# A weighted sum over a large table: two half rows per load instead of one

## Chip, cores and metric

The kernel runs on one core of a Trainium2 chip. The metric is the device time of one execution in microseconds (us). Three timed executions of the kernel before gave a median of 1765.91 us (1764.79 to 1768.8). A separate execution was profiled; its own time stands in the table further down.

## What is computed

One transformer-like block works on 512 tokens of width 1024. Its second half, where the change lies, is a retrieval over 16384 "experts": a row of table `u_tab` and a row of table `v_tab` each, 1024 numbers wide, 64 MB a table. Cut from the reference:

```python
e_idx = ...            # 8 heads x 16 chosen experts per token
gates = jax.nn.softmax(cv, axis=-1)
def one_block(args):
    xi, ei, gi = args
    ue = jnp.take(u_tab, ei, axis=0)
    a = jnp.einsum('thkd,td->thk', ue, xi)
    wgt = (jax.nn.gelu(a.astype(jnp.float32)) * gi).astype(xi.dtype)
    ve = jnp.take(v_tab, ei, axis=0)
    return jnp.einsum('thk,thkd->td', wgt, ve)
```

## The kernel before, in words

For 384 of the 512 tokens the kernel does the retrieval densely. The 128 other tokens get their rows by indirect loads. A table has 128 **chunks** of 128 experts. The *first product* multiplies a chunk of `u_t` with all tokens (PE, TensorE) and gives gelu(u x) in `gelz`. The gates, scattered earlier into a DRAM array `gates_by_key`, come back by loads into `gring` (four chunks a load, 768 KB, line 499). `weigh` (DVE, line 1449) multiplies the two into `wf`. The *second product* multiplies `wf` with the chunk of `v_tab` and adds up in PSUM.

The matmuls work on 32-bit numbers split into a high and a low part. A raw tile is copied to its high part on ACT (`part_v`, line 890, `vhi`; `part_w`, line 882, `eh`), and DVE takes the difference (`low_v`, line 1461, `vlo`; `low_w`, line 1455, `el`). PE then multiplies high by high, low by high and high by low (lines 1629 to 1631).

The second product runs in 16 **groups** g of 8 chunks. PSUM holds only half of the 1024 output columns at a time, so a group does its 8 chunks for the left half of the columns, and then again for the right half. This gives 16 **pieces** n = 0..15 in a group: n = 8 * half + k. A piece needs a tile of 128 experts by 512 columns of `v_tab` (256 KB) and is 9 matmuls on PE. The raw tiles lie in `vraw`, a ring of VR = 4 buffers; `vhi` and `vlo` are rings of 4 too. In groups 0 to 4 PE also does a first product ahead of each of the pieces 0 to 7 (`PRE`, first_product in `group`). From group 5 (`V_GROUP`) on it does sums of indirectly loaded rows instead (`quad`, line 1908, tile `ring`): three of them a group, and four a group in groups 5 and 6. These rows are loaded by POOL (line 654), four loads of 512 KB each time that a quad has freed the buffers.

Each engine takes its own list of instructions in order, and semaphores join them. SP issues nearly all loads; the list is:

- `first_half(g)`: for k = 0..7 the load of piece k; behind the loads of even k a load of `gback` (384 KB, line 507, gelu values that were written out earlier; from group 6 on); behind those of k = 0 and 4 a load of `gring`.
- `second_half(g)`: the loads of pieces 8..15, with the loads of `u_t` for the next group between them as long as there are chunks left.

The `gring` load behind piece 0 of group g, called the **seam load** here, brings the gates of the group's chunks 4 to 7. DVE needs it at `weigh(g, 4)`, which it does already in the second half of group g-1, ahead of `low_v` of piece 1 of group g. In that second half DVE's turn at k is `low_v` of piece k+11 (of piece k-5 of the next group from k = 5 on), `weigh(g+1, k-1)` and `low_w(g+1, k-1)`. Then group g+1 begins on DVE: three additions of PSUM to `acc` (line 1480), `low_w`, `weigh`, `low_w` and `low_v` of piece 3.

The load of piece n may be issued once `low_v` of piece n-4 has read the buffer that it overwrites:

Of the kernel before, what the change touches and what calls it, by code (L numbers as in the profile page):

```python
# [13 lines left out]
P = 128  # L14
D = 1024
# [17 lines left out]
HALF = D // 2  # L33
# [29 lines left out]
CH = NK  # L63
# [22 lines left out]
VR = 4  # L86
# [22 lines left out]
assert [sum(n) for n in LOWS] == [STEPS[0], STEPS[2]] and sum(ONES) * WIDE == P  # L109


def build(nc, x, cb, b_modc, w_modt, wblk, b_fc, conv_wc, conv_vec, keys_t, u_t, u_tab, v_tab, rows, out):
    with ExitStack() as ctx:
        KB = 1024
        base = (nc.sbuf_base + 31) // 32 * 32
# [1 line left out]
        def sb(name, shape, dt, kb):  # L117
            return nc.alloc_sbuf_tensor_at(name, shape, dt, offset=base + int(kb * KB))

        def sem(name):  # L120
            return ctx.enter_context(nc.semaphore(name))
# [55 lines left out]
        vraw = sb("vraw", [P, VR, HALF], F32, 144)  # L177
# [162 lines left out]
        w_mul = sem("w_mul")  # L340
        w_hi = sem("w_hi")
        w_lo = sem("w_lo")
        v_in = [sem(f"v_in{i}") for i in range(VR)]
        v_hi = sem("v_hi")
        v_lo = sem("v_lo")
        v_mm = sem("v_mm")
# [18 lines left out]
        def need(eng, s, value):  # L365

            if value > 0:
                eng.wait_ge(s, value)

        def v_slot(n, last):  # L370

            if last and 8 <= n < 12:
                return vhi2[:, n - 8, :], vlo2[:, n - 8, :]
            return vhi[:, n % VR, :], vlo[:, n % VR, :]

        def v_before(n, last):

            if last and n >= 8:
                return n - 8 if n >= 12 else None
            return n - VR  # L380
# [12 lines left out]
        def chunk(n):  # L393

            return (n + SPILL) % CH
# [17 lines left out]

            return P * q * (q + 1) // 2

        v_half = v_tab.rearrange("(c e) (h d) -> c h e d", e=P, h=2)

        def on_pool(c):

# [11 lines left out]
        def _(sp):  # L431
# [36 lines left out]

            def load_v(g, k, half):
                n, c = half * GR + k, chunk(GR * g + k)  # L470
                need(sp, v_lo, 16 * g + n - VR + 1)
                src = v_half[c, half]
                sp.dma_start(vraw[:, n % VR, :], src).then_inc(v_in[n % VR], 16)

            def store_gel(m):

# [35 lines left out]
            for k in range(VR):  # L512
                load_v(0, k, 0)
# [6 lines left out]
            def first_half(g):  # L520
                for k in range(GR):
                    if g > 0 or k >= VR:
                        load_v(g, k, 0)
                    pr = (GR * g + k) // 2 + 2
                    if k % 2 == 0 and BESIDE * GR // 2 <= pr < CH // 2:
                        load_back(pr)
                    q = (GR * g + k) // 4 + 1
                    if k % 4 == 0 and 2 <= q < CH // 4:
                        load_g(q)

            def second_half(g):
                c = PRE + RAW + GR * g
                for j in range(3):
                    if c + j < CH:
                        load_u(c + j)
                for k in range(GR):
                    load_v(g, k, 1)
                    if k + 3 < GR and c + k + 3 < CH:
                        load_u(c + k + 3)
# [13 lines left out]
            for i, t in enumerate((TD, 0, 1)):  # L553
                sp.wait_ge(y_p, i + 1)
                r = (t + 1) % TT * P
# [109 lines left out]
        def _(act):  # L665
# [39 lines left out]
            for n in range(G0):  # L705
# [19 lines left out]
                elif n < V0 and (n - C0) % 2 == 1:  # L725
                    i = (n - C0) // 2
# [32 lines left out]
            for h in range(HEADS):  # L759
                n = G0 + 2 * h  # L760
# [121 lines left out]
                nc.scalar.activation(eh[:, k, :], wf[:, k % 2, :], ACT.Copy).then_inc(w_hi, 1)  # L882

            def part_v(g, n, last=False):
                act.wait_ge(v_in[n % VR], 16 * (4 * g + n // VR + 1))
                before = v_before(n, last)
                if before is not None:
                    need(act, v_mm, 16 * g + before + 1)
                hi_slot, _ = v_slot(n, last)
                nc.scalar.activation(hi_slot, vraw[:, n % VR, :], ACT.Copy).then_inc(v_hi, 1)  # L890


            for j in range(FILL):
                ahead(SPILL + j)
                if j == 4:
                    for i in range(2):
                        act.wait_ge(stage_out[i], 16 * (LAID * NBT // 16))
                if j >= 4:
                    part_w(j - 4, j - 4)
                if j >= 5:  # L900
                    part_v(0, j - 5)
            gelu(PRE - 1)

            def group(g, last=False):
                for k in range(GR):
                    if k == 0:
                        part_w(GR * g + GR - 1, GR - 1)
                    c = PRE + GR * g + k
                    if k and c < CH:
                        gelu(c - 1)  # L910
                    if c + 2 < CH:
                        part_u(c + 2)
                    part_v(g, k + 3, last)
                    if last and k == 6:
                        root(5, slice(TD, TT))
                if PRE + GR * g < CH:
                    gelu(PRE + GR * g + GR - 1)
                if g == W_GROUP:
                    act.wait_ge(dot_r, SLOTS)
                    nc.scalar.activation(own_a[:], own_a[:], ACT.Gelu_apprx_tanh).then_inc(own_gel, 1)  # L920
                for k in range(GR):
                    if k + 11 < 16:
                        part_v(g, k + 11, last)
                    elif not last:
                        part_v(g + 1, k - 5)
                    if k and not last:
                        part_w(GR * g + GR + k - 1, k - 1)
# [1083 lines left out]
```

## Time and profile before

| | |
|---|---|
| median of three timed executions | 1765.91 us |
| the profiled execution, its own time | 1768.56 us |
| its span, first to last instruction | 1766.3 us |
| mean granted TensorE clock | 0.976 |
| PE busy | 1632.5 us (92%) |
| DVE busy | 1349.7 us (76%) |
| ACT busy | 689.6 us (39%) |
| POOL busy | 642.3 us (36%) |
| second product | about 950 to 1742 us of the span |
| `vraw` loads | 256 of 256 KB, median 6.3 us from issue to landing |
| `gring` loads | 32 of 768 KB, median 10.5 us |

Times in the rows are counted from the start of the span. Idle time of an engine counts only where another engine waits for it; so the rows below go from the engine that is nearly always busy (PE) back to what it waited for.

### The profile page before, as it was taken

How to read it: one execution, taken by the hardware profiler on the slowest of the kernel's cores; microseconds unless marked ns; L12 is line 12 of the kernel's file. 1: busy time of each engine (PE TensorE's matmuls, PEld its weight loads, DVE VectorE, ACT ScalarE, POOL GpSimd, SP SyncE). 2: the span in 40 equal slices, each digit the busy share in tenths (PEclk: the TensorE clock that was granted, in tenths of full speed). 3: DMA queues.
4: the chain of work that ended last, by engine and by line, in shares of the span. 5: the costliest groups of instructions: out<-in, count | busy, mean ns of one | idle time of the engine just before them, and what ended most of it. 6: DMA issues, size and time to landing. Idle time of an engine off the chain costs nothing.

```text
span 1766.3 us, 23113 instructions
## 1 busy us (share of the span) xinstructions
PE 1632.5 (92%) x8238; PEld 1376.3 (78%) x8238; DVE 1349.7 (76%) x2714; ACT 689.6 (39%) x1036; POOL 642.3 (36%) x434
## 2 busy tenths in 40 slices
PE   3998999995999999999887999999989999989996
PEld 3786777774899989898887898898966677656765
DVE  7488776888588999999947998898855556535688
ACT  3334665424333344544533334334233333323332
POOL 2000000002125788767643654653624333322201
PEclk9999999997999999999998999999999999999998
DMA  7414224453665656667677988988979999998962
GB/s 276 155 37 149 90 96 167 143 190 120 239 250 186 169 150 172 179 179 206 188 275 263 392 319 318 389 319 320 332 247 359 343 349 344 344 361 279 347 220 101
DMA packets 194993, 422.28 MB, mean 239 GB/s; under 512 B 33600, under 2 KB 82880, under 8 KB 193856
## 3 DMA queue, kind: packets, MB, share of 16 engines
q1 hardware_dynamic: 137040, 264.47, 43.4%
q0 software_dynamic: 56688, 139.55, 23.8%
q10 hardware_dynamic: 1152, 16.78, 2.3%
q8 instruction: 67, 1.10, 0.2%
q14 instruction: 46, 0.38, 0.1%
HBM read 375.55 MB, written 45.15 MB: 238 GB/s over the span
## 4 chain that ended last, share of the span: by engine, by line
PE 61%; DVE 23%; DMA 9%; ACT 3%; issue 2%; SPq 1%; DVEq 0%; ACTq 0%
PE bank L1629 18%; PE bank L1630 18%; PE bank L1631 18%; DMA gring<-gates_by_key 5%; DMA vraw<-in_v_tab_dram 2%; PE bank L1908 2%; DVE wlo L1268 2%; DVE one L1419 2%; DVE one L1421 2%; DVE one L1423 2%; DVE wf L1449 1%; PE bank L1722 1%; DVE raw L958 1%; PE bank L1707 1%; DVE vlo L1461 1%
## 5 line engine op out<-in xcount | busy, mean ns | idle before, releaser
L1629 PE MATMUL bank<-act_hi,whi 128*128 128x384 f32 (+1 forms) x1352 | 484.1, 358 | 30.0 <-ACT gelz L839 11.8
L1630 PE MATMUL bank<-act_lo,whi 128*128 128x384 f32 (+1 forms) x1352 | 474.2, 351 | 0.0
L1631 PE MATMUL bank<-act_hi,wlo 128*128 128x384 f32 (+1 forms) x1352 | 474.1, 351 | 0.0
L1629 PE MATMUL bank<-vhi,eh 128*128 128x512 f32 x768 | 309.2, 403 | 25.2 <-DVE vlo L1461 25.2
L1630 PE MATMUL bank<-vlo,eh 128*128 128x512 f32 x768 | 304.1, 396 | 0.0
L1631 PE MATMUL bank<-vhi,el 128*128 128x512 f32 x768 | 303.3, 395 | 0.0
L1629 PEld LDWEIGHTS bank<-act_hi,whi 128*128 128x128 f32 x1352 | 257.0, 190 | 50.6 <-issue 18.6
L1461 DVE TENSOR_TENSOR vlo<-vraw,vhi 128x512 fp32r<-128x512 f32 x256 | 174.6, 692 | 129.5 <-ACT vhi L890 129.1
L1630 PEld LDWEIGHTS bank<-act_lo,whi 128*128 128x128 f32 x1352 | 256.9, 190 | 14.2
L1631 PEld LDWEIGHTS bank<-act_hi,wlo 128*128 128x128 f32 x1352 | 256.3, 190 | 13.4
L629 POOL DMA_INDIRECT gates_by_key<-selW,selS x128 | 238.6, 1864 | 71.0 <-issue 45.3
L613 POOL DMA_INDIRECT ring<-in_u_tab_dram,idxN x128 | 188.5, 1472 | 179.9 <-DVE ring L1273 137.8
L654 POOL DMA_INDIRECT ring<-in_v_tab_dram,idxT x128 | 133.6, 1043 | 296.9 <-PE bank L1908 265.2
L890 ACT ACTIVATE vhi<-vraw 128x512 fp32r<-128x512 f32 x256 | 157.5, 623 | 196.1 <-DMA vraw<-in_v_tab_dram 110.1
L1629 PEld LDWEIGHTS bank<-vhi,eh 128*128 128x128 f32 x768 | 145.9, 190 | 88.8 <-DVE vlo L1461 38.8
L1631 PEld LDWEIGHTS bank<-vhi,el 128*128 128x128 f32 x768 | 146.3, 190 | 32.0
L1630 PEld LDWEIGHTS bank<-vlo,eh 128*128 128x128 f32 x768 | 146.4, 191 | 28.4 <-issue 0.2
L1268 DVE TENSOR_TENSOR wlo<-raw,whi 128x1024 fp32r<-128x1024 f32 x108 | 132.6, 1233 | 46.8 <-ACT whi L830 46.5
L882 ACT ACTIVATE eh<-wf 128x384 fp32r<-128x384 f32 x128 | 67.2, 525 | 238.5 <-DVE wf L1449 238.5
L1273 DVE SCALAR_TENSOR_TENSOR ring<-ring,x2s 128x1024 f32<-128x1024 f32 x128 | 151.3, 1222 | 6.7 <-DMA ring<-in_u_tab_dram,idxN 6.3
L839 ACT ACTIVATE gelz<-bank 128x384 f32<-128x384 f32 x128 | 63.1, 493 | 234.4 <-PE bank L1631 234.4
L830 ACT ACTIVATE whi<-raw 128x1024 fp32r<-128x1024 f32 x128 | 134.5, 1053 | 20.8 <-DMA raw<-in_u_t_dram 20.8
(230 smaller groups left out, 2014.5 us busy)
## 6 DMA issues: line engine op xcount, KB each, us to landing
raw<-in_u_t_dram SPq DMA_DIRECT2D x128, 512.0 KB, 5.3
vraw<-in_v_tab_dram SPq DMA_DIRECT2D x256, 256.0 KB, 6.3
raw<-in_wblk_dram SPq DMA_DIRECT2D x61, 512.0 KB, 4.2
raw<-in_w_modt_dram SPq DMA_DIRECT2D x48, 512.0 KB, 4.2
gring<-gates_by_key SPq DMA_DIRECT2D x32, 768.0 KB, 10.5
gates_by_key<-stage ACTq DMA_DIRECT2D x8, 2048.0 KB, 7.8
gelu_ahead<-gelz SPq DMA_DIRECT2D x20, 768.0 KB, 4.2
gback<-gelu_ahead SPq DMA_DIRECT2D x40, 384.0 KB, 7.7
```

The lines of the kernel that those rows point to most:

```text
L613: pool.indirect_dma_start(out=ring[:, j % RING, :], out_offset=None, in_=u_tab, in_offset=bass.IndirectOffsetOnAxis(ap=idxN[:, j:j + 1], a ...
L629: pool.indirect_dma_start(out=gates_flat, out_offset=bass.IndirectOffsetOnAxis(ap=selS[:, n:n + 1], axis=0), in_=selW[:, n:n + 1], in_offs ...
L654: pool.indirect_dma_start(out=ring[:, n % RING, :], out_offset=None, in_=v_tab, in_offset=bass.IndirectOffsetOnAxis(ap=idxT[:, tok:tok + 1 ...
L830: nc.scalar.activation(whi[:, c % SPL, :], raw[:, c % RAW, :], ACT.Copy).then_inc(u_hi, 1)
L882: nc.scalar.activation(eh[:, k, :], wf[:, k % 2, :], ACT.Copy).then_inc(w_hi, 1)
L890: nc.scalar.activation(hi_slot, vraw[:, n % VR, :], ACT.Copy).then_inc(v_hi, 1)
L1268: nc.vector.tensor_tensor(wlo[:, c % SPL, :], raw[:, c % RAW, :], whi[:, c % SPL, :].bitcast(F32), ALU.subtract).then_inc(u_lo, 1)
L1273: nc.vector.scalar_tensor_tensor(out=ring[:, j % RING, :], in0=ring[:, j % RING, :], scalar=1.0, in1=x2s[:], op0=ALU.mult, op1=ALU.mult, a ...
L1461: nc.vector.tensor_tensor(lo_slot, vraw[:, n % VR, :], hi_slot.bitcast(F32), ALU.subtract).then_inc(v_lo, 1)
L1629: mm(o, wh, mh, start=start, stop=False)
L1630: mm(o, wh, ml, start=False, stop=False)
L1631: return mm(o, wl, mh, start=False, stop=stop)
```

## The change

The second table is given to the kernel in another layout, `v_pair` (made on the host). A partition row of it has the left (or right) half row of expert e in chunk 2m and, right behind it, the same half row of expert e in chunk 2m+1. One load therefore brings the tiles of two pieces, n and n+1 with n even, into two neighbouring buffers of `vraw`: 512 KB, 4 KB a partition. There are 128 such loads instead of 256. One semaphore stands for a pair of buffers, so `part_v` of either piece waits for the whole pair. The load waits until both buffers are free: for `low_v` of piece n-3, where piece n waited for piece n-4 and piece n+1 for piece n-3. `v_tab` stays for the indirect loads.

```diff
-        v_in = [sem(f"v_in{i}") for i in range(VR)]
+        v_in = [sem(f"v_in{i}") for i in range(VR // 2)]
...
-        v_half = v_tab.rearrange("(c e) (h d) -> c h e d", e=P, h=2)
...
             def load_v(g, k, half):
                 n, c = half * GR + k, chunk(GR * g + k)
-                need(sp, v_lo, 16 * g + n - VR + 1)
-                src = v_half[c, half]
-                sp.dma_start(vraw[:, n % VR, :], src).then_inc(v_in[n % VR], 16)
+                if k % 2 == 0:
+                    need(sp, v_lo, 16 * g + n - VR + 2)
+                    sp.dma_start(vraw[:, n % VR:n % VR + 2, :], v_pair[c // 2, half].rearrange("e (r d) -> e r d", r=2)
+                                 ).then_inc(v_in[n % VR // 2], 16)
...
             def part_v(g, n, last=False):
-                act.wait_ge(v_in[n % VR], 16 * (4 * g + n // VR + 1))
+                act.wait_ge(v_in[n % VR // 2], 16 * (4 * g + n // VR + 1))
...
+        "v_pair": a["peer_v"][0].reshape(CH // 2, 2, P, 2, HALF).transpose(0, 3, 2, 1, 4).reshape(CH // 2, 2, P, D),
```

SP's list around the seam of two late groups, before. The first row is the `gback` load behind piece 6; the ten loads behind it are pieces 7 to 15 and piece 0 of the next group:

```order
L507 DMA gback<-gelu_ahead 128x768 [waits gel_out0,w_mul,u_mm]
L473 DMA vraw<-in_v_tab_dram 128x512 [waits v_lo] x10
L507 DMA gback<-gelu_ahead 128x768 [waits gel_out1,w_mul,u_mm]
L499 DMA gring<-gates_by_key 128x12x128 [waits w_mul]
L473 DMA vraw<-in_v_tab_dram 128x512 [waits v_lo] x2
L507 DMA gback<-gelu_ahead 128x768 [waits gel_out1,w_mul,u_mm]
```

The same place in the changed kernel; the five loads are the pairs (8, 9) to (14, 15) and (0, 1) of the next group:

```order
L507 DMA gback<-gelu_ahead 128x768 [waits gel_out0,w_mul,u_mm]
L472 DMA vraw<-in_v_pair_dram 128x1024 [waits v_lo] x5
L507 DMA gback<-gelu_ahead 128x768 [waits gel_out1,w_mul,u_mm]
L499 DMA gring<-gates_by_key 128x12x128 [waits w_mul]
L472 DMA vraw<-in_v_pair_dram 128x1024 [waits v_lo]
L507 DMA gback<-gelu_ahead 128x768 [waits gel_out1,w_mul,u_mm]
```

Piece 1 has moved from behind the seam load to ahead of it, and the seam load itself now stands behind a load that waits for `low_v` of piece 13 of the group before, where it stood behind one that waits for that of piece 12. In the same way piece 5 moves ahead of the second `gring` load of a group. The end of SP's list, before; the thirteen loads are pieces 3 to 15 of the last group:

```order
L473 DMA vraw<-in_v_tab_dram 128x512 [waits v_lo] x2
L507 DMA gback<-gelu_ahead 128x768 [waits gel_out1,w_mul,u_mm]
L473 DMA vraw<-in_v_tab_dram 128x512 [waits v_lo] x13
L556 DMA out_dram<-xfin 128x1024 [waits y_p] x3
L560 DMA out_dram<-xfin 128x512 [waits y_r] x2
```

The end in the changed kernel, with the pairs (4, 5) to (14, 15) as the six loads:

```order
L472 DMA vraw<-in_v_pair_dram 128x1024 [waits v_lo]
L507 DMA gback<-gelu_ahead 128x768 [waits gel_out1,w_mul,u_mm]
L472 DMA vraw<-in_v_pair_dram 128x1024 [waits v_lo] x6
L556 DMA out_dram<-xfin 128x1024 [waits y_p] x3
L560 DMA out_dram<-xfin 128x512 [waits y_r] x2
```

The last load of all now brings pieces 14 and 15 together. The lists of PE, DVE and ACT are the same as before, instruction by instruction.

## Rows read from the trace of the kernel before

**Rows 1.** Page, part 1 (busy us, share) and part 4 (shares of the chain)

```profile
PE 1632.5 (92%) x8238; PEld 1376.3 (78%) x8238; DVE 1349.7 (76%) x2714; ACT 689.6 (39%) x1036; POOL 642.3 (36%) x434
PE 61%; DVE 23%; DMA 9%; ACT 3%; issue 2%; SPq 1%; DVEq 0%; ACTq 0%
```

**Rows 2.** Busy time by stretch: four stretches of the second product

```profile
core 0: us, PE busy (x) PEld busy (x) DVE busy (x) ACT busy (x) POOL busy (x), PEclk, DMA share, GB/s
960.00:1280.00 320.00, 318.17 (x1602) 289.70 (x1603) 285.21 (x457) 117.95 (x191) 178.41 (x120) 0.99 0.92 340
...
1440.00:1480.00 40.00, 38.90 (x196) 27.96 (x192) 22.00 (x38) 12.80 (x24) 11.77 (x12) 1.00 0.98 343
...
1680.00:1720.00 40.00, 39.57 (x192) 27.88 (x192) 32.52 (x55) 11.86 (x21) 4.00 (x4) 1.00 0.67 226
...
1442.00:1457.00 15.00, 15.00 (x75) 10.97 (x74) 7.98 (x14) 4.82 (x10) 5.95 (x7) 1.00 1.01 348
```

**Rows 3.** Waits, 960 to 1766 us: us in total, times, longest

```profile
PE bank L1629 <- DVE vlo L1461: 25.2, 15, 5.2
...
DVE wf L1449 <- DMA gring<-gates_by_key: 29.1, 13, 6.4
```

**Rows 4.** Instructions of tile vraw, 1280 to 1720 us

```profile
  DMA vraw<-in_v_tab_dram: 103.6, 38
...
DMA to landing us min/median/max: 2.5/6.6/22.3
```

**Rows 5.** Timeline of SP, 1437 to 1454 us: start, length

```profile
1444.39 0.37 SPq L507 DMA_DIRECT2D gback<-gelu_ahead  x1
1444.80 0.67 SPq L499 DMA_DIRECT2D gring<-gates_by_key  x1
1446.22 5.41 SPq L473 DMA_DIRECT2D vraw<-in_v_tab_dram  x2
```

**Rows 6.** Timeline of DVE, 1443 to 1467 us, with idle time before

```profile
1450.05 0.69 DVE L1461 TENSOR_TENSOR vlo<-vraw,vhi 128x512 fp32r<-128x512 f32 x1
...
1452.32 0.69 DVE L1461 TENSOR_TENSOR vlo<-vraw,vhi 128x512 fp32r<-128x512 f32 x1
1456.41 0.56 DVE L1449 TENSOR_TENSOR wf<-gback,gring 128x384 f32<-128x384 f32 x1 [3.40 <-DMA gring<-gates_by_key]
...
1465.35 1.29 DVE L1461 TENSOR_TENSOR vlo<-vraw,vhi 128x512 fp32r<-128x512 f32 x2
```

**Rows 7.** Timeline of PE, first and last of seven waits at piece 3

```profile
1295.01 0.80 PE L1629 MATMUL bank<-vhi,eh 128*128 128x512 f32 x1 [4.94 <-DVE vlo L1461]
...
1680.24 0.50 PE L1629 MATMUL bank<-vhi,eh 128*128 128x512 f32 x1 [0.77 <-DVE vlo L1461]
```

**Rows 8.** Packets by queue: 1398 to 1401 us (q1), 1444 to 1457 us (q0)

```profile
q1 hardware_dynamic: 225, 0.42, 39.1%
...
q0 software_dynamic: 540, 1.95, 41.2%
```

**Rows 9.** Chain that ended last, two loads; PE's waits, 1320 to 1400 us

```profile
1328.74 15.82 DMA vraw<-in_v_tab_dram
...
1372.24 16.20 DMA vraw<-in_v_tab_dram
...
PE bank L1629 <- DVE vlo L1461: 4.0, 2, 2.5
```

**Rows 10.** Chain that ended last, from the last load on

```profile
1736.69 2.55 DMA vraw<-in_v_tab_dram
1739.26 0.64 ACT vhi L890
1739.93 0.69 DVE vlo L1461
```

**Rows 11.** Last seam load: its issue (SP), its landing, and DVE's use

```profile
1702.50 0.43 SPq L499 DMA_DIRECT2D gring<-gates_by_key  x1
...
DMA to landing us min/median/max: 6.9/6.9/6.9
...
1710.63 0.55 DVE L1449 TENSOR_TENSOR wf<-gback,gring 128x384 f32<-128x384 f32 x1
```

More of the change, by code:

```diff
@@ L109, with build @@
 assert [sum(n) for n in LOWS] == [STEPS[0], STEPS[2]] and sum(ONES) * WIDE == P
-def build(nc, x, cb, b_modc, w_modt, wblk, b_fc, conv_wc, conv_vec, keys_t, u_t, u_tab, v_tab, rows, out):
+def build(nc, x, cb, b_modc, w_modt, wblk, b_fc, conv_wc, conv_vec, keys_t, u_t, u_tab, v_tab, v_pair, rows, out):
     with ExitStack() as ctx:
```

## Prediction

> **What bounds the kernel now.** I read the page first. PE is busy 92% of the span, and the chain that ended last runs over PE for 61%, over DVE for 23% and over DMA for 9% [rows 1]. So a change of loads can take away only what PE waits for, and can cost whatever it makes PE wait for in addition. The table by stretches shows two kinds of second product. From 960 to 1280 us PE also has the first products and is busy 318 of 320 us. From there on it is busy 38.9 of 40 us in a typical late group, and the DMA engines are full: a share of 0.98 in the late group, and 1.01 at 348 GB/s in the 15 us around the seam at 1442 to 1457 us. Only in the last stretch, when the indirect loads have run out, does the share fall to 0.67 [rows 2].
>
> The waits say what ends last. PE waited for `vlo` 15 times, 25.2 us in all, and DVE waited 13 times, 29.1 us, for a `gring` load at `weigh` [rows 3]. ACT waited 38 times for a raw half row, 103.6 us [rows 4]; that is much more than PE waited, so most of these waits are covered by pieces that PE still has in hand.
>
> The seam near 1457 us shows how the two are joined. SP issues the seam load at 1444.80, behind piece 0, and piece 1 only behind it [rows 5]. DVE ends `low_v` of piece 0 at 1453.0 and then sits 3.40 us until the seam load has landed; from `weigh` at 1456.41 to `low_v` of piece 3 at 1465.35 it works through its list without a gap worth naming [rows 6]. PE waits for just that piece 3. Seven of PE's 15 waits are at piece 3 behind a seam load that DVE waited for: the first, of 4.94 us, at 1295.01, the last, of 0.77 us, at 1680.24 [rows 7]. At these seven a seam load that lands later by x makes PE later by x. At the seams of groups 1 to 4, PE has first products of more than 6 us a piece before it, so nothing follows there.
>
> **The change part by part.** *128 issues fewer on SP.* An issue that isn't held up takes 0.4 us or so [rows 5], and SP is no engine that others wait for except through its waits: worth 0. If SP were the limit it would be 0.4 us a pair.
>
> *Bytes and packets.* The bytes are the same. A packet of 2 KB took 39.1% x 16 x 3 us / 225 = 0.083 us, a 4 KB packet of the indirect loads 41.2% x 16 x 13 us / 540 = 0.159 us [rows 8]. If a 4 KB packet on SP's queue takes 0.159, a pair needs 8 x (2 x 0.083 - 0.159) = 0.06 us less on each engine. In a late group that is 0.5 us of DMA time in 40 us: below what shows, taken as 0, bounds -0.5 us a group and 0.
>
> The Trainium skill (DMA: Bandwidth & Descriptors, Bandwidth) advises loads of at least 1 MiB and gives each a fixed cost of about 2 us; 128 loads fewer would then be 256 us less, if they ran one behind the other. The trace disagrees with such a sum: several loads are in flight, and PE's waits for `vlo` are 25.2 us in all [rows 3].
>
> *The seam load comes later.* It stands behind a wait for `low_v` of piece 13 where it was piece 12, and these are 1452.32 - 1450.05 = 2.27 us apart in DVE's rhythm [rows 6]; and 256 KB more (piece 1) go ahead of it in the same queue, which at 348 GB/s [rows 2] is 0.75 us. Does the 2.27 us count? With the DMA engines full, the time in which SP has nothing queued is used by the indirect loads, which then are out of the way earlier; the seam load ends when the sum of the work ahead of it is done. So x is 0.75 us if the engines stay full, and 0.75 + 2.27 = 3.0 us if they don't. Below 0.75 it can fall only if the larger packets gain on the indirect loads (a rival below). The nearest row is the share of 1.01 at a seam, so I take 0.75: seven seams make +5.2 us, bounds 0 and 21.
>
> *The last seam.* Here the share is only 0.67 [rows 2]. The seam load was issued at 1702.50, landed 6.9 us later at 1709.4, and was used at 1710.63 [rows 11]: 1.2 us in hand, 3.0 us later: +1.8 us, bounds 0 and 3. Behind it DVE's list leads to the end.
>
> *The other pieces.* Piece 5 no longer queues behind the second `gring` load of a group. In two groups that was a load of 15.8 and 16.2 us on the chain, and PE's two waits in 1320 to 1400 us were 4.0 us [rows 9]. But pieces 6 and 7 still stand behind the `gring` load and follow at once, so part of the wait moves on to them. I take half: -2 us, bounds -4 and 0. Even pieces elsewhere come one piece later than now: 2.27 us, where PE works through the stock of pieces ahead (a piece is 9 matmuls, some 2 us). 15 waits of PE over 240 pieces say that this stock is seldom empty; taken as 0, at most a few tenths at the ends of the right halves in groups 0 to 4. The loads of `u_t` move by one piece of more than 6 us in a ring of four: 0. What stands behind SP's longer waits, the `gback` loads, moves like the seam load and has been counted with it.
>
> *The end.* The last load was issued at 1736.69 and landed 2.55 us later; then ACT 0.64, DVE 0.69, all on the chain [rows 10]. Now it carries pieces 14 and 15: 0.75 us more to land, and DVE has both pieces to do behind it, 0.69 more: +1.4 us, bounds 0.7 and 2.
>
> Sum: 5.2 + 1.8 - 2 + 1.4 = +6.4 us. The profiled execution took 1768.6 us (its span 1766.3 and 2.3 around it), so it would take 1775.0. The median of the three timed runs stands 2.65 us below the profiled one; on it the sum gives 1772.3, and I forecast **1772 us**.
>
> **The rivals.**
> *The whole step counts.* If DMA engines run dry for the 2.27 us, x is 3.0 us at seven seams: 21 + 1.8 - 2 + 1.4 = +22 us, 1788. For it: the indirect loads come in bursts of four, and between bursts the engines may be idle; against it the share of 1.01 at the seam [rows 2].
>
> *Faster: larger packets win against the indirect loads.* If an engine takes one packet of each queue in turn, two half rows cost 16 x (0.083 + 0.159) = 3.9 us beside indirect loads, and a pair 8 x (0.166 + 0.159) = 2.6 us [rows 8]. Ahead of the seam load three or four pieces stand so: pieces 14, 15 and 0 took 3 x 8 x 0.242 = 5.8 us, the pairs (14, 15) and (0, 1) take 5.2, so the seam load comes 0.6 us earlier instead of 0.75 later: -4.2 us, with both waits of [rows 9] gone -4.0, and +1.8 and +1.4 as before: -5.0 us, 1760.9. It decides if the indirect loads are still running when the seam load's own packets begin; if they have ended, nothing is won, since the sum of work is the same.
> The Trainium skill (DMA: Bandwidth & Descriptors, Queues, rings and completion order) states this rule: an engine goes round its queues packet by packet. By that rule the time would be the 1760.9 us of this rival. The trace doesn't contradict it, but both queues' shares in the 13 us [rows 8] do not show whose packets came first.
>
> *No change.* The seam load's landing is that of its slowest engine, and 0.75 us may vanish in it; then seams 0, last seam 0, pieces -2, end +1.4: -0.6 us, 1765.3. The same result comes out if the seams cost 5.2 and piece 5 gives back all 4.0.
>
> **How the numbers follow.** Forecast with its own spread (1769.5 to 1779): 0.43. The whole step, or most of it: 0.17. No change: 0.21. Faster: 0.19. The range reaches down to the rival with larger packets and up to where half of the whole step's cases lie: 1761 to 1786 us; the likeliest case alone has 1769.5 to 1779. A measurement of this kernel can tell 0.2%, 3.5 us, from no change. Slower by more than that: 0.43 + 0.17 = 0.60; within: 0.21; faster: 0.19.
>
> **What the profile after would show.** DVE's wait for `gring` grows from 29.1 us by 5 to 8 us if I am right, by 20 or more if the whole step counts, and falls if the larger packets win. The seam load issues some 2 us later against the start of its second half, and lands under 1 us later. PE's waits for `vlo` grow at piece 3 of groups 5 and 8 to 14, and those of 1320 to 1400 us shrink from 4.0 us. The DMA share in the late groups stays near 0.98. At the end, two `low_v` follow the last load. I am wrong if the seam load's landing against PE isn't what moves, above all if PE begins to wait for even pieces, which now come with their odd neighbour.

## The result, and the profile after

The changed kernel took 1800.21 us (median of four; 1796.84 to 1801.18), the kernel before 1766.16 us beside it (1764.79 to 1768.8). The ratio is 1.0188, 95% interval 1.017 to 1.0205: slower by 34 us, where +6.4 was forecast. The profiled execution has a span of 1798.8 us against 1766.3.

The page of the changed kernel: part 1, the two largest queues of part 3, and the shares of the chain that ended last:

```profile
PE 1636.7 (91%) x8238; PEld 1374.6 (76%) x8238; DVE 1350.6 (75%) x2714; ACT 688.7 (38%) x1036; POOL 634.7 (35%) x434
...
q1 hardware_dynamic: 118608, 264.47, 42.3%
q0 software_dynamic: 56688, 139.55, 23.4%
...
PE 39%; DVE 30%; DMA 17%; issue 5%; POOL 4%; ACT 4%; SPq 1%; DVEq 0%; ACTq 0%
```

The engines do the same work as before, and PE's share of the chain has fallen from 61% to 39% [rows 1], in favour of DVE and DMA: PE now waits more often. The waits of 960 to 1800 us (us in total, times, longest), answering to [rows 3]:

```profile
PE bank L1629 <- DVE vlo L1461: 48.3, 25, 4.9
...
DVE wf L1449 <- DMA gring<-gates_by_key: 25.4, 10, 5.6
```

PE's waits for `vlo` grew by 23.1 us. Of the 32.5 us by which the span is longer, 28.3 are idle time of PE and 4.2 more busy time. DVE's wait for `gring`, which I expected to grow, shrank. The table by stretches of the changed kernel, answering to [rows 2]; groups 0 to 4 fill the first row, and the late groups come 16 to 28 us later than before, so equal times are not equal work:

```profile
core 0: us, PE busy (x) PEld busy (x) DVE busy (x) ACT busy (x) POOL busy (x), PEclk, DMA share, GB/s
960.00:1280.00 320.00, 309.41 (x1543) 279.53 (x1544) 274.77 (x437) 112.58 (x181) 170.16 (x116) 0.99 0.88 325
...
1440.00:1480.00 40.00, 35.33 (x168) 24.47 (x168) 19.76 (x34) 11.84 (x21) 10.97 (x12) 0.96 0.88 304
1680.00:1720.00 40.00, 38.07 (x185) 27.55 (x177) 29.08 (x48) 12.16 (x22) 12.02 (x12) 1.00 0.94 334
```

PE lost time even where it has first products. The DMA share of 0.88 at 1440 to 1480 us is that of one stretch; over the same work, groups 5 to 14, it was 0.93 at 326 GB/s before (1280 to 1710 us) and 0.89 at 314 GB/s after (1296 to 1737 us), for about the same bytes in a longer time. To see where the time arose I compared the start of `low_v` of the same piece in the two timelines of DVE. Piece 0 of group 5 started at 1280.0 before and 1296.4 after, piece 0 of group 15 at 1710.0 and 1737.5, the last piece at 1739.9 and 1772.5. So on DVE **16.5 us arose in groups 0 to 4, 11 in groups 5 to 14, 5 in the last group**. Part of the first number is time that `low_v` had in hand ahead of PE: PE's own first matmul of the same three pieces came 14.1, 27.5 and 32.7 us later. These three places are the measure of the experiments below.

**One place in full: the end of group 0.** The kernel before, pieces 14 and 15: SP's load of piece 14 (the first of the row), DVE's `low_v` of 14, and PE's first matmul of 14:

```profile
998.66 7.90 SPq L473 DMA_DIRECT2D vraw<-in_v_tab_dram  x3
...
1010.06 0.69 DVE L1461 TENSOR_TENSOR vlo<-vraw,vhi 128x512 fp32r<-128x512 f32 x1
...
1013.06 0.39 PE L1629 MATMUL bank<-vhi,eh 128*128 128x512 f32 x1
```

The same in the changed kernel: the pair (14, 15), ACT's copy of piece 14, `low_v`, and PE:

```profile
1007.65 3.27 SPq L472 DMA_DIRECT2D vraw<-in_v_pair_dram  x2
...
1014.74 0.63 ACT L890 ACTIVATE vhi<-vraw 128x512 fp32r<-128x512 f32 x1 [3.15 <-DMA vraw<-in_v_pair_dram]
...
1015.40 0.69 DVE L1461 TENSOR_TENSOR vlo<-vraw,vhi 128x512 fp32r<-128x512 f32 x1 [3.22 <-ACT vhi L890]
...
1016.15 0.50 PE L1629 MATMUL bank<-vhi,eh 128*128 128x512 f32 x1 [2.02 <-DVE vlo L1461]
```

Before, piece 14 was ready 2.3 us before PE took it, and PE didn't wait. The pair is issued 9.0 us later than the single load was, and lands 7.1 us behind its issue; ACT, DVE and PE then wait one behind the other. Of the 9.0 us, 2.0 are lateness that DVE already had at piece 11, and 7.0 are the step from `low_v` of piece 10 to `low_v` of piece 11, which is 7.0 us in each of groups 0 to 4 and not the 2.27 us of DVE's rhythm that the prediction took from a late seam. In between DVE has the low part of a `u_t` chunk (line 1268), three dot products of indirectly loaded rows (line 1273) and three copies out of PSUM (line 1478; additions, line 1480, in later groups).

The wait also costs time behind it: from 1017 to 1020 us the granted TensorE clock was 0.50, its lower level of 1.2 GHz, and the matmuls of piece 14 began 0.43 us apart instead of 0.23. PE was idle for 2.02 us just before. From its first matmul of group 0 to that of group 5 PE took 346.8 us instead of 332.9; of these 13.9 us, 8.6 are waits for `vlo` and 4.4 more busy time.

### The profile page after: what moved, and what is told of

Same layout as the page of the kernel before. It is cut to its first block, busy times and chain, and to the rows that moved or that the text cites. A ratio compares the mean times of both kernels' runs of the same rounds, so it can differ in the third digit from the quotient of the medians.

```text
span 1798.8 us, 22985 instructions
## 1 busy us (share of the span) xinstructions
PE 1636.7 (91%) x8238; PEld 1374.6 (76%) x8238; DVE 1350.6 (75%) x2714; ACT 688.7 (38%) x1036; POOL 634.7 (35%) x434
## 3 DMA queue, kind: packets, MB, share of 16 engines
q1 hardware_dynamic: 118608, 264.47, 42.3%
## 4 chain that ended last, share of the span: by engine, by line
PE 39%; DVE 30%; DMA 17%; issue 5%; POOL 4%; ACT 4%; SPq 1%; DVEq 0%; ACTq 0%
PE bank L1629 11%; PE bank L1630 11%; PE bank L1631 11%; DMA vraw<-in_v_pair_dram 6%; DMA gring<-gates_by_key 6%; POOL ring L613 4%; DVE wlo L1268 3%; DMA ring<-in_u_tab_dram,idxN 3%; DVE vlo L1461 2%; DVE wf L1449 2%; DVE one L1419 2%; DVE one L1421 2%; DVE one L1423 2%; DVE el L1455 2%; ACT eh L882 1%
## 5 line engine op out<-in xcount | busy, mean ns | idle before, releaser
L1629 PE MATMUL bank<-act_hi,whi 128*128 128x384 f32 (+1 forms) x1352 | 483.2, 357 | 31.8 <-ACT gelz L839 11.8
L1461 DVE TENSOR_TENSOR vlo<-vraw,vhi 128x512 fp32r<-128x512 f32 x256 | 173.8, 691 | 160.1 <-ACT vhi L890 159.6
L1630 PEld LDWEIGHTS bank<-act_lo,whi 128*128 128x128 f32 x1352 | 256.2, 190 | 14.1
L613 POOL DMA_INDIRECT ring<-in_u_tab_dram,idxN x128 | 183.7, 1435 | 199.0 <-DVE ring L1273 158.1
L1630 PEld LDWEIGHTS bank<-vlo,eh 128*128 128x128 f32 x768 | 147.3, 192 | 28.3 <-issue 0.2
L1273 DVE SCALAR_TENSOR_TENSOR ring<-ring,x2s 128x1024 f32<-128x1024 f32 x128 | 151.6, 1220 | 11.9 <-DMA ring<-in_u_tab_dram,idxN 11.7
```

The lines of the kernel that those rows point to most:

```text
L613: pool.indirect_dma_start(out=ring[:, j % RING, :], out_offset=None, in_=u_tab, in_offset=bass.IndirectOffsetOnAxis(ap=idxN[:, j:j + 1], a ...
L1273: nc.vector.scalar_tensor_tensor(out=ring[:, j % RING, :], in0=ring[:, j % RING, :], scalar=1.0, in1=x2s[:], op0=ALU.mult, op1=ALU.mult, a ...
L1461: nc.vector.tensor_tensor(lo_slot, vraw[:, n % VR, :], hi_slot.bitcast(F32), ALU.subtract).then_inc(v_lo, 1)
L1629: mm(o, wh, mh, start=start, stop=False)
L1630: mm(o, wh, ml, start=False, stop=False)
```

## The experiments

Each kernel was timed against the kernel before on the same chip, which took 1764.2 to 1766.8 us in these comparisons. The last three columns are how much later than in the kernel before `low_v` started in the profiled execution, at piece 0 of group 5, at piece 0 of group 15, and at the last piece. These columns are rough. The change, e2, e13 and e15 are the same kernel up to group 5 and stand there at +12.8 to +16.5; the change and e15 are the same up to group 15 and differ by 6.3 there. The profiled execution of the kernel before was 2.4 us above its own median, and for all kernels but e7 the last column lies 0.7 to 8.6 us below the difference of the medians.

| kernel | median us (range) | ratio [95%] | g 5 | g 15 | last |
|---|---|---|---|---|---|
| the change | 1800.2 (1796.8–1801.2) | 1.0188 [1.017, 1.0205] | +16.5 | +27.5 | +32.5 |
| e1 two singles | 1786.0 (1783.8–1794.2) | 1.0131 [1.009, 1.0171] | +10.5 | +12.1 | +15.8 |
| e8 joint wait | 1800.1 (1799.6–1801.6) | 1.0198 [1.0175, 1.0221] | +10.1 | +30.6 | +33.0 |
| e14 joint, not at 0 and 4 | 1785.0 (1782.4–1790.6) | 1.011 [1.0081, 1.0139] | +3.6 | +11.7 | +13.8 |
| e7 pair, 2 KB rows | 1804.2 (1796.3–1808.8) | 1.0204 [1.0164, 1.0244] | +19.3 | +35.7 | +40.3 |
| e2 pairs in groups 0–4 | 1777.3 (1775.3–1778.0) | 1.0066 [1.0047, 1.0085] | +13.7 | +7.5 | +6.6 |
| e3 pairs from group 5 | 1781.0 (1778.0–1784.0) | 1.0094 [1.0061, 1.0127] | +0.5 | +5.5 | +9.5 |
| e15 last group single | 1790.0 (1789.2–1793.3) | 1.0134 [1.0111, 1.0157] | +14.0 | +21.2 | +20.5 |
| e4 seam load first | 1806.3 (1802.8–1809.4) | 1.0227 [1.0202, 1.0252] | +16.8 | +36.9 | +40.9 |
| e6 early seam, pair | 1816.8 (1812.0–1822.2) | 1.0304 [1.0276, 1.0331] | +20.9 | +40.3 | +43.5 |
| e5 early seam, single | 1772.3 (1764.8–1780.5) | 1.0038 [1.002, 1.0055] | +0.4 | +0.6 | +0.9 |
| e9 short dots, single | 1757.6 (1753.4–1760.3) | 0.9959 [0.9944, 0.9974] | −6.7 | −12.3 | −12.9 |
| e10 short dots, pair | 1775.1 (1769.8–1777.3) | 1.0056 [1.004, 1.0072] | −6.1 | +0.6 | +4.9 |
| e11 eight buffers, single | 1744.2 (1742.7–1744.6) | 0.988 [0.9858, 0.9902] | +0.5 | −24.8 | −24.4 |
| e12 eight buffers, pair | 1745.8 (1745.5–1746.4) | 0.9889 [0.9867, 0.9912] | +0.9 | −22.0 | −21.6 |
| e13 pairs, eight from 6 on | 1757.4 (1756.4–1759.6) | 0.9953 [0.9932, 0.9974] | +12.8 | −11.0 | −10.7 |

### Which half of the pair costs: the request or the landing

A pair does two things at once: it is requested only when both buffers are free, and neither piece can be used before both have landed. The first kernel keeps single loads of 256 KB with semaphores of their own, but issues both where the pair is issued:

```diff
-                need(sp, v_lo, 16 * g + n - VR + 1)
-                src = v_half[c, half]
-                sp.dma_start(vraw[:, n % VR, :], src).then_inc(v_in[n % VR], 16)
+                if k % 2 == 0:
+                    need(sp, v_lo, 16 * g + n - VR + 2)
+                    for i in range(2):
+                        sp.dma_start(vraw[:, n % VR + i, :], v_half[c + i, half]).then_inc(v_in[n % VR + i], 16)
```

> The loads of before (256 KB, 2 KB a partition, a semaphore each), but issued two and two when the buffers of both pieces are free, in the order of the changed kernel. Theory W (the later issue costs the time): about as slow as the changed kernel, +28 to +36 us. Theory S (the size of the load costs it: the even piece also waits for the bytes of the odd one, and 4 KB packets press on the indirect loads): +0 to +12 us.

It took 1786.0 us, some 21 of the 34 us, between what the two theories expected, and two thirds of its delay arose in groups 0 to 4. So the late request by itself is dear. The other half was tried in the kernel before, its loads and issues untouched, with one wait more on ACT:

```diff
                 act.wait_ge(v_in[n % VR], 16 * (4 * g + n // VR + 1))
+                if n % 2 == 0:
+                    act.wait_ge(v_in[n % VR + 1], 16 * (4 * g + n // VR + 1))
```

> The kernel before, loads and issue times unchanged, but ACT's copy of an even piece also waits for the load of the odd piece behind it. This is the joint landing alone. As the two singles issued together gave +21 us of the +34, theory S expects +8 to +16 us here, half of it in groups 0 to 4. If the rest of the +34 was in the size of the load as such (how it shares the DMA engines): below +4.

1800.1 us, 35 above the kernel before, far over what both theories expected, and with e1's 21 more than the whole change. That sum showed a flaw of this experiment: piece 1 stands behind the seam load in SP's list and piece 5 behind the second `gring` load, so here pieces 0 and 4 waited for those too, which they don't in the changed kernel. The next kernel leaves these two out (`if n % 2 == 0 and n not in (0, 4)`).

> The kernel before with its own loads and issue times; ACT's copy of an even piece also waits for the odd one's load, except at pieces 0 and 4, whose odd neighbours stand behind a gring load. If joint landing by itself is dear, 8 us at group 5 as in the kernel that waits at all pairs and 30 us or more in all. If most of that kernel's cost in the late groups was the seam load put ahead of piece 0, still 6 to 10 us at group 5 but at most 8 more behind it: 1771 to 1782 us.

1785.0 us, above the 1771 to 1782 expected: 18 us over the kernel before, so that some 15 of e8's 35 us were the wait behind the `gring` loads. At group 5 it stands at +3.6, below the 6 to 10 expected, and behind it 10 us were added.

The two experiments aren't two separate halves, though. Among single loads the odd piece's is issued just where the pair would be, behind `low_v` of piece n-3. An even piece that waits for it (e14) is therefore as late as one whose own load is issued there (e1). The traces show it: at piece 14 of groups 0 to 4 ACT waits for a half row 0 us in the kernel before, 11.4 in e1, 12.0 in e14 and 16.0 in the change. By their medians e1 and e14 give 20.8 + 18.2 = 39.0 us, more than the 34 of the change. So they don't divide the 34 us. What they show is that it costs 18 to 21 us if an even piece is ready only once a load issued one piece later has landed, with loads of 256 KB too. With equal waits of ACT at piece 14, e1 lost 10.5 us before group 5 and e14 3.6; DVE's waits for its own indirect loads there are 10.6 us in e1 and 5.3 in e14 (6.3 before). Why those differ is open.

### Packets

One load for two pieces as in the change, but out of the old layout, so that its packets stay at 2 KB:

```diff
-                    sp.dma_start(vraw[:, n % VR:n % VR + 2, :], v_pair[c // 2, half].rearrange("e (r d) -> e r d", r=2)
+                    sp.dma_start(vraw[:, n % VR:n % VR + 2, :], v_two[c // 2, :, half].rearrange("r e d -> e r d")
```

> The changed kernel, but its one load per pair takes the two half rows from the old table, so that its packets are 2 KB again. If the packet size matters (4 KB packets take more from the indirect loads on which DVE's dot products wait in groups 0 to 4): 5 to 15 us faster than the changed kernel. Theory W and the joint landing alone: within 4 us of the changed kernel, +30 to +38 us over before.

1804.2 us, with an interval that overlaps that of the change. The larger packets aren't what costs. They may give up to a few us, but these runs don't tell that from nothing. What they save on the engines is near the prediction's estimate: SP's queue took 42.8% of 1806.6 us in e7 and 42.3% of 1798.8 in the change, some 12 us less for each engine, where 0.06 us a pair make 8.

The Trainium skill (DMA: Bandwidth & Descriptors, Queues, rings and completion order) says that an engine goes round its queues packet by packet. It means by a packet a bundle of typically 9 to 17 descriptors, while the packets counted in the rows here are of 2 or 4 KB each; so the time of 1760.9 us that the prediction gave "by that rule" doesn't follow from the rule alone, and no run here shows whose packets came first.

### Where: groups, seams, the end

> Pairs in groups 0 to 4 only, single loads from group 5 on. From the two traces, in which low_v of piece 0 of group 5 comes 16 us later: +14 to +18 us over before. If the delay there were taken back later by waits that exist anyway: below +8.

> Pairs from group 5 on only. By difference of the traces: +14 to +18 us over before. The recorded forecast, which placed nearly all of its cost here, would give +6. If the parts do not add up (the early delay changes how the later loads meet the indirect ones), the sum of this and the last kernel differs from +34 by more than 6.

Here `load_v` issues pairs in some groups and single loads in the others. Pairs in groups 0 to 4 alone cost 12 us, less than the 14 to 18 expected, pairs from group 5 on 16 us: 28 of the 34. In e2 the timelines show +13.7 at group 5 and +6.6 at the last piece, but its median is 12.1 us above the kernel before; so how much of the early loss is given back where single loads follow, 2 us or 7, isn't settled. In e3 nothing is lost before group 5 (+0.5). The prediction had all its cost in the late groups.

The theory of the prediction, that the seam load's lateness is what costs, was tried by issuing `gback` and `gring` of k = 0 ahead of the pair (0, 1), and in two further kernels by issuing them in the right half before, behind piece 10:

```diff
                 for k in range(GR):
-                    if g > 0 or k >= VR:
+                    if k and (g > 0 or k >= VR):
                         load_v(g, k, 0)
...
+                    if k == 0 and g > 0:
+                        load_v(g, 0, 0)
```

> The changed kernel with one thing moved: in each group from the second on, SP issues the gback and gring loads of k = 0 ahead of the pair (0, 1) and so ahead of its wait for low_v of piece 13. Theory L (the seam load, now later, is what costs time from group 5 on): DVE's wait for gring falls from 37 us to below 25, and the kernel is 6 to 12 us faster than the changed one. Theory W+S (the half rows themselves are late everywhere): within 4 us of the changed kernel, or slower, since the pair (0, 1) now stands behind 1.1 MB.

> The changed kernel, with the gback and gring loads of k = 0 issued already in the right half of the group before, behind piece 10. Theory L: DVE's wait for gring at the seams is gone, 10 to 16 us faster than the changed kernel, the rest of its +34 stays in groups 0 to 4 and at the end. W+S: under 5 us faster.

> The kernel before with the same move of the gback and gring loads, single loads as before. DVE waited 29.1 us for gring and PE waited at piece 3 of seven groups behind it; if the seam load is the cause of these waits of PE, 5 to 12 us faster than before. If another load or DVE's list takes its place: within 3 us of before.

Theory L misses in all three; e4 and e6 fall on the side of W+S, and e5, 7.6 us slower, was expected by neither theory. (The 37 us in e4's text count one wait of 11.6 us ahead of group 0 besides the 25.4 above.) In none of the three DVE waits for `gring` any more, and none is faster: with pairs 1806.3 and 1816.8 us, in the kernel before 1772.3. The wait moves on to the raw half rows that now stand behind 768 KB, from group 6 on behind 384 KB of `gback` too. DVE's waits at `low_v` for ACT's copy, those included that the profile puts down to "issue", are 129.1 us in the kernel before and 157.0 in e5: 28 us more for the 29.1 us at `gring` that are gone. Four of them, 5.7 to 6.5 us each, and one of 2.7 us are at piece 11, whose load now stands right behind the moved ones. In the changed kernel they are 159.6 us, in e4 194.8 and in e6 195.3. The theory falls: a seam load that comes first only makes the half rows behind it late.

For the end, the changed kernel with single loads in the last group:

> The changed kernel with single loads in the last group alone. If the 5 us lost in the last half group belong to the last loads: 1794 to 1797 us, against 1800. If they are lost time from before that only shows there: 1798 to 1802.

1790.0 us, 10 less than the change and below both ranges. In the last group it lost nothing (+21.2 to +20.5), where the change lost 5.0 (+27.5 to +32.5); the other half of its gain arose before that group, where the two kernels are the same, and stays unexplained. The chain of the changed kernel shows the place. Its first row here is the end of `low_v` of piece 3:

```profile
1750.94 0.67 DVE vlo L1461
1751.63 3.18 DMA vraw<-in_v_pair_dram
...
1767.27 0.61 DVE vlo L1461
1767.90 3.27 DMA vraw<-in_v_pair_dram
1771.19 0.64 ACT vhi L890
1771.86 1.29 DVE vlo L1461 x2
```

The pair (6, 7) has to wait for `low_v` of piece 3, and in DVE's list that stands behind six sums (lines 1494 and 1501); as a single load piece 6 would go behind `low_v` of piece 2, some 7 us earlier. The last two rows are the end that the prediction described: 0.7 us for the longer load and 0.6 for the second `low_v` against [rows 10].

### Why groups 0 to 4: DVE's full list

DVE's waits in groups 0 to 4 show where its time goes (us in total, times, longest). Before, 939 to 1280 us:

```profile
DVE vlo L1461 <- ACT vhi L890: 6.6, 8, 0.9
DVE ring L1273 <- DMA ring<-in_u_tab_dram,idxN: 6.3, 10, 1.3
```

In the changed kernel, 939 to 1296 us:

```profile
DVE vlo L1461 <- ACT vhi L890: 20.9, 10, 3.7
DVE ring L1273 <- DMA ring<-in_u_tab_dram,idxN: 11.7, 13, 1.4
```

At `low_v` it waits 14.3 us more, at its own dot products 5.4 us more, and 3.4 us at `gring` are gone: 16.3 us, as much as `low_v` of group 5 comes later. Its busy time is the same, so on DVE nothing of the lateness was taken up by idle time.

If PE is hit there because DVE has no time left to catch up, a shorter list on DVE must take the cost away with the pairs' lateness left in place. Both kernels here take the dot products over 128 of 1024 columns, and leave out the rest of the sum:

```diff
-                nc.vector.scalar_tensor_tensor(out=ring[:, j % RING, :], in0=ring[:, j % RING, :], scalar=1.0,
-                                               in1=x2s[:], op0=ALU.mult, op1=ALU.mult,
+                nc.vector.scalar_tensor_tensor(out=ring[:, j % RING, 0:P], in0=ring[:, j % RING, 0:P], scalar=1.0,
+                                               in1=x2s[:, 0:P], op0=ALU.mult, op1=ALU.mult,
```

> The kernel before with DVE's own dot products taken over 128 of the 1024 columns; the indirect loads stay as they are, the rest of each dot product is left out. It is the base for the same edit in the changed kernel. DVE was busy 285 of 320 us in groups 0 to 4 and PE waited there for less than 10 us in the kernel before, so all theories expect little here: 1755 to 1766 us.

> The changed kernel with the same short dot products (the rest of each is left out). Theory F, DVE's full list makes the pair dear in groups 0 to 4: low_v of piece 0 of group 5 comes at most 4 us later than in the kernel before with short dots (16.5 us later with whole ones), and the time is 16 to 24 us above that kernel instead of 34. Rival B, the pair is dear because it holds half of the four buffers and its request comes too late, whatever DVE has to do: 12 us or more at group 5, and 28 to 38 us in all.

The pair now costs 17.6 us in all instead of 34, 0.6 at group 5 instead of 16.5, and behind it 12.3 and 4.9 us, as in the change (11 and 5). The two kernels by stretch and by ACT's waits, 960 to 1280 us, first with single loads:

```profile
960.00:1280.00 320.00, 320.00 (x1613) 290.39 (x1612) 179.68 (x449) 117.54 (x191) 119.42 (x118) 1.00 0.92 343
...
ACT vhi L890 <- DMA vraw<-in_v_tab_dram: 0.4, 1, 0.4
```

and with pairs, with `low_v` of piece 14 of group 0 as the last row:

```profile
960.00:1280.00 320.00, 320.00 (x1613) 290.03 (x1612) 178.57 (x449) 117.51 (x191) 120.17 (x118) 1.00 0.90 340
...
ACT vhi L890 <- DMA vraw<-in_v_pair_dram: 11.8, 4, 3.5
...
1005.88 0.69 DVE L1461 TENSOR_TENSOR vlo<-vraw,vhi 128x512 fp32r<-128x512 f32 x1 [3.42 <-ACT vhi L890]
```

ACT still waits for pairs, 11.8 us in four waits, where the changed kernel has 16.0 in five over the same groups, and DVE waits behind it, 3.42 us at this piece. But DVE is busy 179 of 320 us instead of 275, has its pieces ready early, and PE is busy for all of the 320 us. So in groups 0 to 4 the price is lateness times a full list on DVE.

### Buffers

If the late request costs because a pair holds half of four buffers, it must cost nothing with eight. From group 6 on `gelz` and `x2s` are dead and give room for four more raw buffers:

```diff
+        vraw2 = sb("vraw2", [P, VR, HALF], F32, 96)
...
+                if g < DEEP:
+                    need(sp, v_lo, 16 * g + n - VR + 1)
+                    sp.dma_start(raw_v(g, n), v_half[c, half].unsqueeze(1)).then_inc(v_in[n % VR], 16)
+                    return
+                lag = VR if g == DEEP and n < VR else 2 * VR
...
+                need(sp, v_lo, 16 * g + n - lag + 1)
+                sp.dma_start(raw_v(g, n), v_half[c, half].unsqueeze(1)).then_inc(v_deep[n % (2 * VR)], 16)
```

> The kernel before, but from group 6 on it has eight raw buffers instead of four (over gelz and x2s, which are dead by then), so that a load is issued up to eight pieces ahead. If the late landings of raw half rows and of the seam load bound the late groups, 5 to 15 us faster than before (1750 to 1760). If the DMA engines' full share bounds them, the same: 1763 to 1768.

> Single loads in groups 0 to 5, the changed kernel's pairs from group 6 on, with eight raw buffers there, so that a pair is issued with three pairs still ahead of it. With four buffers, pairs from group 5 on cost 16 us. Theory B, request and landing are late because a pair holds half of the buffers: within 4 us of the kernel with eight buffers and single loads. Rival Q, it is the load of 512 KB in the queue itself that costs: 9 us or more above it.

1744.2 and 1745.8 us: the pair costs 1.6 us from group 6 on, where with four buffers it cost 16 us from group 5 on (e3), and **both kernels are faster than the kernel before, by 20 and 18 us**. With single loads, waits of 960 to 1800 us and three stretches:

```profile
PE bank L1643 <- DVE vlo L1475: 9.9, 5, 4.9
...
DVE wf L1463 <- DMA gring<-gates_by_key: 8.7, 6, 3.4
...
1400.00:1440.00 40.00, 40.00 (x198) 28.87 (x197) 22.87 (x40) 14.23 (x26) 12.32 (x13) 1.00 1.05 370
1440.00:1480.00 40.00, 40.00 (x198) 28.88 (x197) 23.29 (x41) 13.77 (x25) 12.59 (x13) 1.00 1.02 361
1480.00:1520.00 40.00, 40.00 (x198) 28.84 (x198) 22.84 (x40) 13.84 (x25) 12.52 (x12) 1.00 1.00 350
```

and with pairs:

```profile
PE bank L1645 <- DVE vlo L1477: 10.5, 6, 4.2
...
DVE wf L1465 <- DMA gring<-gates_by_key: 12.6, 7, 4.5
...
1440.00:1480.00 40.00, 40.00 (x198) 28.89 (x197) 23.29 (x41) 13.77 (x25) 12.59 (x13) 1.00 0.98 350
```

PE is busy 40.00 of 40 us in stretch after stretch, and its waits for `vlo` are 9.9 us where they were 25.2 [rows 3]. The DMA engines move 370 GB/s where the kernel before moved 325 at 1400 to 1440 us, so the late groups weren't bound by their full share. These two kernels don't tell the late request from a dearer transfer, since a deeper ring would hide either; but a pair takes no longer from issue to landing than a single load did (median 6.1 us against 6.3), and e1 and e14 are slow with loads of 256 KB. The last kernel has pairs in all groups and eight buffers from group 6 on:

> Pairs in all groups, with eight raw buffers from group 6 on and four before. If the parts add up: 1744 us for eight buffers with single loads, the 12 to 16 us that pairs cost in groups 0 to 4, and 1.5 for pairs from group 6 on: 1757 to 1762 us. If the deeper ring gives the lost time back: 1744 to 1750.

1757.4 us, 1745.8 plus the 12 of e2: the parts add up.

## Why the prediction was wrong

The direction was right, the size was not, and most of the loss came by a step that the sum held at nothing.

- **The step that failed: "The other pieces … taken as 0, at most a few tenths at the ends of the right halves in groups 0 to 4".** The right halves of groups 0 to 4 cost 12 us of the time (e2), 14.1 us on PE's timeline. The step rested on two readings. The delay was taken as one turn of DVE, 2.27 us [rows 6], from a seam in the late groups; at the end of a right half in groups 0 to 4 the turn has dot products and copies or additions in it and takes 7.0 us. And the stock was judged by a count over the kernel, 15 waits in 240 pieces [rows 3] (there are 256), not by the time that the single piece is ready ahead of PE; at piece 14 that is 2.3 us in group 0 and 3.1 to 4.0 in groups 1 to 4, less than the 7.0. The condition written at the prediction's end, that PE begins to wait for even pieces, is what happened: of its waits in groups 0 to 4 (8.6 us in six), four are at piece 14, 7.3 us, and two at piece 11, 1.3 us.
- **The same step in the late groups.** There too even pieces come late, and there the term was 0 as well. In group 8 ACT waits 3.60 us for the pair (14, 15) of the group before and 1.89 us for the pair (2, 3), in group 11 3.14 us for (14, 15); before it waited at none of these. DVE stands still behind these copies.
- **The seams.** The reading of seven seams was wrong. DVE did not wait for a seam load at group 5: PE's 4.94 us there [rows 7] come from DVE's first work for the quads (lines 1577 to 1586), and stay 4.93 us in the changed kernel. Such a wait stood at six seams, piece 3 of groups 8, 9, 11, 13 and 14 and piece 1 of group 12; with 0.75 us each that is 4.5 and not 5.2. At these six places PE waited 9.7 us before and 14.0 after: +4.3, so the size fits. The mechanism does not: DVE's wait for `gring` fell from 29.1 to 25.4 us. In groups 8 and 11 it fell from 3.36 and 2.77 us to 0.20 and 0.51, while PE's wait at piece 3 grew from 1.07 and 1.32 us to 3.27 and 3.38. And with the seam load issued earlier the kernels got slower.
- **The last seam, +1.8**, came as told: DVE waited 1.85 us for this load, where it hadn't waited before, and PE's wait at piece 3 of group 15 grew from 2.44 to 4.39 us.
- **Piece 5, −2.** Nothing came back. PE's waits in groups 6 and 7 were 4.0 us before [rows 9] and are 4.0 after (1338 to 1425 us). In groups 5 to 14 ACT had waited 43.4 us at piece 5, and now waits 41.4 us at piece 6.
- **The end, +1.4.** The last load and its two `low_v` cost 1.3, as worked out. But the last group lost 5 us: besides these 1.3 and the 2 of the last seam, its pairs come late as elsewhere, with both buffers to wait for and DVE's sums in between.
- **Issues, packets, `u_t` loads, 0.** No run speaks against packets at 0 (e7). The `u_t` loads were not tried by themselves.
- **The rival "the whole step counts"** had +22 us by a seam load that comes 3.0 us later while DMA engines run dry. The share in groups 5 to 14 did fall, from 0.93 to 0.89, but it is the half rows that come late and not the seam load. That rival, too, had nothing for groups 0 to 4, and 1800 lies beyond its 1788.

That the direction came out right is in part luck: most of the loss arose where the prediction expected none. Left open: why the parts of e2 and e3 give 28 and not 34 (perhaps some giving back behind group 5 in e2), how the 34 us divide between late request and joint landing, and the 6 us by which e15 is better before its last group.

## What to carry to other kernels

A load that serves two steps is requested when the later buffer comes free and delivers when the later byte lands: count both against the number of buffers. Here room for two merged loads was too little and room for four was enough; three weren't tried. Take the delay from the place where the consumer's turn is longest, and compare it there with the time that the piece lies ready before it is needed; an average over the kernel hides the few places that decide. When ACT or DVE wait for loads although the DMA engines look full, try more buffers before larger transfers.

## What the runs showed that was not expected

- A DMA share of 0.95 to 1.00 didn't mean that no more could be moved. With eight buffers and single loads (e11) the late groups ran at 350 to 388 GB/s and a share of 1.00 to 1.05, where the kernel before had 325 to 366 at 0.95 to 1.00 in the same stretches (1360 to 1560 us).
- The Trainium skill advises loads of at least 1 MiB (DMA: Bandwidth & Descriptors, Bandwidth). Both sizes here lie below that, so no run here tests it; but a step towards it gained nothing in this ring. 512 KB instead of 256 KB cost 34 us with four buffers, 16 of them from group 5 on, and 1.6 us with eight from group 6 on.
- Moving one load of 768 KB a group forward in its queue, with the `gback` load beside it, took away the 29.1 us of waits for it and left the time 0.4% longer (e5), as 28 us of other waits took their place.
- SP's issue of a load right behind a `gring` load was held up. In the kernel before, that of piece 1 lasted 2.1 to 4.9 us in 13 of groups 1 to 14 and 16.2 us in group 12, that of piece 9 0.33 us in every group. In the changed kernel the pair (2, 3) stands in that place, issued later against the `gring` load: 0.33 us in 14 of 16 groups, and 12.6 in group 12.
